# Gathering expert rows: h in PSUM, the dot products shared out over three engines, and the picks chosen between dots

## The reference

```python
def peer_ffn(h, wq, keys, u, v):       # u, v: (16384, 2048)
    q = (xt @ wq).reshape(-1, 8, 2, 128)
    s = jnp.einsum('thpc,hpnc->thpn', q, keys)
    sv, si = lax.top_k(s, 16)
    cand = (sv[:, :, 0, :, None] + sv[:, :, 1, None, :]).reshape(-1, 8, 256)
    cid = (si[:, :, 0, :, None] * 128 + si[:, :, 1, None, :]).reshape(-1, 8, 256)
    top_s, top_j = lax.top_k(cand, 16)
    eid = jnp.take_along_axis(cid, top_j, axis=-1)
    gate = jax.nn.softmax(top_s, axis=-1)
    ue = jnp.take(u, eid, axis=0)
    act = jax.nn.gelu(jnp.einsum('thkd,td->thk', ue, xt), approximate=False)
    ve = jnp.take(v, eid, axis=0)
    return jnp.einsum('thk,thkd->td', gate * act, ve)
```

## Time and profile before

| | us |
|---|---|
| median of 3 runs | 3186.89 (3186.21 to 3187.88) |
| the profiled execution, its own time | 3189.3 |
| its span, first to last instruction | 3187.6 |
| first gather of u issued | 1815.94 |
| first dot starts | 1835.04 |
| last dot's result read | 2576.1 |
| steady matmuls of the v stage from | 2644.8 |

### The profile page before, as it was taken

The page is one execution under the profiler, slowest core; times in us unless marked ns, Lnnn a source line. Parts: engine busy times, 40 slices in busy tenths (PEclk is TensorE's granted clock), DMA queues, the critical chain, the costliest instruction groups (busy, mean ns, idle before and its releaser), DMA issues.

```text
span 3187.6 us, 33891 instructions
## 1 busy us (share of the span) xinstructions
PE 2394.3 (75%) x10945; PEld 2000.4 (63%) x10945; DVE 2242.5 (70%) x2950; ACT 1111.3 (35%) x1197; POOL 763.3 (24%) x548
## 2 busy tenths in 40 slices
PE   7999999999999998999998900000111149999997
PEld 5888888888888886888886700000111147887885
DVE  4456455555444556455656699999999998888888
ACT  4444344444444543343443300000000024444443
POOL 1000000000000000000000076665565614455543
PEclk8999999999999998899999955555555589999998
DMA  7655555555656354555564498888897928999996
GB/s 246 195 186 185 178 179 191 185 192 185 185 185 185 124 194 139 164 162 166 187 221 155 172 403 369 362 362 354 316 379 306 391 78 294 320 317 331 322 323 230
DMA packets 183123, 766.51 MB, mean 240 GB/s; under 512 B 22172, under 2 KB 22224, under 8 KB 149104
## 3 DMA queue, kind: packets, MB, share of 16 engines
q1 hardware_dynamic: 123232, 415.29, 40.3%
q0 software_dynamic: 59792, 349.90, 28.0%
HBM read 763.00 MB, written 2.10 MB: 240 GB/s over the span
## 4 chain that ended last, share of the span: by engine, by line
PE 69%; DVE 22%; issue 5%; DMA 2%; ACT 1%; DVEq 1%; POOL 0%; SPq 0%; ACTq 0%; POOLq 0%
PE half L604 50%; PE half L945 15%; DVE ring L1853 14%; DVE onehot_a L1840 2%; PE half L623 1%; DMA w_raw<-in_a_w_in 1%; DMA v_raw<-in_peer_v 1%; DVE onehot_b L1836 1%; PE half L800 1%; DVEq L1840 0%; PE half L672 0%; DMA v_rows<-in_peer_v,idx 0%; DVE left L1751 0%; PE half L903 0%; DVE onehot L1794 0%
## 5 line engine op out<-in xcount | busy, mean ns | idle before, releaser
L604 PE MATMUL half<-w_split,xT 128*128 128x512 f32 x7104 | 1639.0, 392 | 15.2 <-DVE xT L1302 12.6
L604 PEld LDWEIGHTS half<-w_split,xT 128*128 128x128 f32 x7104 | 1337.9, 189 | 294.5 <-issue 8.6
L1283 DVE TENSOR_TENSOR w_split<-w_raw,w_split 128x1024 fp32r<-128x1024 f32 x592 | 722.5, 1225 | 764.1 <-ACT w_split L985 763.3
L985 ACT ACTIVATE w_split<-w_raw 128x1024 fp32r<-128x1024 f32 x592 | 626.6, 1059 | 943.4 <-PE half L604 914.1
L564 POOL DMA_INDIRECT ring<-in_peer_u,idx x256 | 480.9, 1879 | 439.5 <-DVE dots L1853 186.2
L1853 DVE CUSTOM_DVE_ANT_0 ring<-ring,h 128x2048 f32<-128x2048 f32 x256 | 570.0, 2285 | 5.0 <-issue 2.5
L945 PE MATMUL half<-v_split,w_x 128*128 128x512 f32 x2304 | 526.8, 391 | 6.1 <-ACT v_split L1235 4.4
L945 PEld LDWEIGHTS half<-v_split,w_x 128*128 128x128 f32 x2304 | 434.4, 189 | 98.3 <-issue 5.6
L929 PE MATMUL half<-onehot_a,onehot_b 128*128 128x128 f32 x512 | 94.9, 361 | 334.9 <-DVE onehot_a L1840 334.9
L578 POOL DMA_INDIRECT v_rows<-in_peer_v,idx x256 | 266.7, 1042 | 330.2 <-DVE h L1917 208.5
L929 PEld LDWEIGHTS half<-onehot_a,onehot_b 128*128 128x128 f32 x512 | 87.8, 267 | 342.2 <-DVE onehot_a L1840 342.2
(11 more groups left out here) (287 smaller groups left out, 1152.8 us busy)
## 6 DMA issues: line engine op xcount, KB each, us to landing
w_raw<-in_a_w_in SPq DMA_DIRECT2D x192, 512.0 KB, 3.5
v_raw<-in_peer_v SPq DMA_DIRECT2D x256, 384.0 KB, 5.4
w_raw<-in_b_w_in SPq DMA_DIRECT2D x128, 512.0 KB, 3.5
w_raw<-in_w_in SPq DMA_DIRECT2D x112, 512.0 KB, 3.5
w_raw<-in_a_w_out SPq DMA_DIRECT2D x64, 512.0 KB, 3.5
w_raw<-in_b_w_out SPq DMA_DIRECT2D x32, 512.0 KB, 4.3
w_raw<-in_w_out SPq DMA_DIRECT2D x32, 512.0 KB, 4.6
w_raw<-in_peer_wq SPq DMA_DIRECT2D x32, 512.0 KB, 4.3
```

What stands on the lines that cost most here:

```text
L604: last = mm(ps[half][:, 2 * t + n, :], xt[:, xp, kk, tok], w_split[:, s, wp, n * BANK:(n + 1) * BANK], start=(k == 0 and xp == 0 and wp == ...
L985: fn(w_split[:, k % SPLIT_SLOTS, 0, :], w_raw[:, k % RAW_SLOTS, :], ACT.Copy).then_inc(hi_done, 1)
L1283: v.tensor_tensor(w_split[:, s, 1, :], w_raw[:, k % RAW_SLOTS, :], w_split[:, s, 0, :].bitcast(F32), ALU.subtract).then_inc(split_done, 1)
```

## The change

It does these things to the gather stage:

- ACT copies `h` of tile 0 into `flat[B]` and of tile 1 into `flat[A]` (`h_copied`), and the dots on DVE read `h` there (new L1911). They write their sums straight to `wgt`; `dots`, `idx`, `stage` and their copies are gone.
- Of each batch of 8, rows 3 and 7 (`POOL_ROWS`) are no longer DVE's. POOL multiplies the row by `h` in SBUF (`scale_row`, new L580, 128 x 2048 f32, both inputs in SBUF), and ACT sums the product (`sum_row`, new L1228). DVE has the six others.
- POOL's queue is written out: four gathers, a `scale_row`, four gathers, a `scale_row`. The gathers read the row numbers in place in `eid`. The gather into slot 3 or 7 waits for ACT's sum of that slot, those of the others for DVE's dot.
- `choosing(n + 1)` is cut into nine pieces that stand between the dots of group n, and `finish_gate(n + 1)` follows the dot at place 21. DVE's casts and constant-operand steps in it are written as TENSOR_TENSOR with a table of constants (`ones`, `halving`).
- The one-hots beside tile 1 come once in each batch, after its second row; `onehot_a` is made by SCALAR_TENSOR_TENSOR there. The scatter products of both tiles go into half B. Keys and weights are turned together (`picks0`, `picks1`). The last quarter of `h` is weighed by ACT (`weigh_h`).

The core of the diff:

```diff
+BATCHES = PICKS // GATHER_SLOTS
+POOL_ROWS = (3, 7)
+DVE_ROWS = tuple(s for s in range(GATHER_SLOTS) if s not in POOL_ROWS)
...
-            BODY = 2 * GATHER_SLOTS
-            with pool.Fori(0, TILES * PICKS // BODY) as i:
-                for n in range(BODY):
-                    b, s = divmod(n, GATHER_SLOTS)
-                    if s == 0:
-                        pool.wait_ge(idx_ready[b], i + 1)
-                    if s == GATHER_SLOTS // 2:
-
-                        pool.wait_ge(products, CHUNKS)
-
-                    pool.wait_ge(rows_used, i * BODY + (n + 1))
+            def gather_u(r):
+
+                s = r % GATHER_SLOTS
+                if r % GROUP_PICKS == 0:
+                    pool.wait_ge(chosen, r // GROUP_PICKS + 1)
+                if r == GATHER_SLOTS // 2:
+                    pool.wait_ge(products, CHUNKS)
+                if r >= GATHER_SLOTS:
+                    j = r // GATHER_SLOTS - 1
+                    if s in POOL_ROWS:
+                        pool.wait_ge(rows_summed, j * len(POOL_ROWS) + POOL_ROWS.index(s) + 1)
+                    else:
+                        pool.wait_ge(rows_used, j * len(DVE_ROWS) + DVE_ROWS.index(s) + 1)
+                pool.nop(nofuse=True)
+                nc.gpsimd.indirect_dma_start(
+                    out=ring[:, s, :], out_offset=None, in_=peer_u_2[0],
+                    in_offset=bass.IndirectOffsetOnAxis(ap=eid[:, r:r + 1], axis=0),
+                ).then_inc(row_landed[s], 16)
+
+            def scale_row(j, s):
+
+                pool.wait_ge(row_landed[s], j * 16 + 16)
+                nc.gpsimd.tensor_tensor(ring[:, s, :], ring[:, s, :], h[:, j // BATCHES, :], ALU.mult)\
+                    .then_inc(rows_scaled, 1)
+
+            for r in range(GATHER_SLOTS):
+                gather_u(r)
+            for j in range(TILES * BATCHES):
+                s = 0
+                for last in POOL_ROWS:
+                    scale_row(j, last)
+                    while s <= last:
+                        if j + 1 < TILES * BATCHES:
+                            gather_u((j + 1) * GATHER_SLOTS + s)
+                        s += 1
...
+            is_emptied(act, "peer_q1")
+            fn(flat[B], h[:, 0, :], ACT.Copy).then_inc(h_copied, 1)
             scores_out(1)()
+            is_emptied(act, "scores1")
+            fn(flat[A], h[:, 1, :], ACT.Copy).then_inc(h_copied, 1)
+
+            def sum_row(j, s):
+
+                r = j * GATHER_SLOTS + s
+                act.wait_ge(rows_scaled, j * len(POOL_ROWS) + POOL_ROWS.index(s) + 1)
+                fn(ring[:, s, :], ring[:, s, :], ACT.Copy, accum_out=wgt[:, r:r + 1]).then_inc(rows_summed, 1)
...
+            def dot_rows(n, at):
+
+                t = n // TILE_GROUPS
+                for k in range(GROUP_PICKS):
+                    r = n * GROUP_PICKS + k
+                    j, s = divmod(r, GATHER_SLOTS)
+                    if s in DVE_ROWS:
+                        dve.wait_ge(row_landed[s], 16 * j + 16)
+                        v.tensor_tensor_reduce(out=ring[:, s, :], in0=ring[:, s, :], in1=flat[1 - t], scale=1.0,
+                                               scalar=0.0, op0=ALU.mult, op1=ALU.add,
+                                               accum_out=wgt[:, r:r + 1]).then_inc(rows_used, 1)
+                    for job in at.get(k, ()):
+                        job()
...
             for n in range(GROUPS_IN_ALL):
+                t, q = divmod(n, TILE_GROUPS)
+                at = {}
                 if n + 1 < GROUPS_IN_ALL:
-                    choose(n + 1)
+                    there, a_first, a_next, pairs, b_first, b_next, exps, key_a, key_b, ids = choosing(n + 1)
+                    at = {1: [there, a_first], 4: [a_next], 6: [pairs], 8: [b_first], 10: [b_next], 12: [exps, key_a],
+                          16: [key_b], 18: [ids], 21: [lambda: finish_gate(n + 1)]}
...
+                if t == 1:
+                    for m in range(P // SCATTER):
+                        group, k = divmod(9 + 8 * m if m + 1 < P // SCATTER else PICKS - 4, GROUP_PICKS)
```

More of the change, by code:

```diff
@@ L563, in _ @@
+            pool.wait_ge(keys_known, TILES)
+            for t in range(TILES):
+                for r in range(t * PICKS, (t + 1) * PICKS):
+                    pool.wait_ge(v_used, r + 1)
                     pool.nop(nofuse=True)
                     nc.gpsimd.indirect_dma_start(
-                        out=ring[:, s, :], out_offset=None, in_=peer_u_2[0],
-                        in_offset=bass.IndirectOffsetOnAxis(ap=idx[:, b, s:s + 1], axis=0),
-                    ).then_inc(row_landed[s], 16)
@@ L569, in _ @@
[L569 to L582 removed]
+                        out=v_rows[r % V_SLOTS][:, :], out_offset=None,
@@ L935, in _ @@
                 pe.wait_ge(keys_known, t + 1)
-                turn_picks(f"pkT{t}", [pick_keys[:, t, half, :] for half in range(2)])
                 pe.wait_ge(wgt_done, t + 1)
-                turn_picks(f"wgtT{t}", [wgt[:, t * PICKS:(t + 1) * PICKS]])
+                turn_picks(f"picks{t}", [pick_keys[:, t, half, :] for half in range(2)]
+                           + [wgt[:, t * PICKS:(t + 1) * PICKS]])
+                emptied(f"picks{t}")()
                 scatter(t)
@@ L1807, in choosing @@
                         + best16(cand, cand_left, tops, topj, GROUP_HEADS)
-                        + [exponents, look_up(0, a, ALU.logical_shift_right, 4), look_up(1, b, ALU.bitwise_and, TOPK - 1),
+                        + [exponents, look_up(0, a, ALU.logical_shift_right), look_up(1, b, ALU.bitwise_and),
                            experts])
-            def choose(n):
-                for part in choosing(n):
-                    part()
             def finish_gate(n):
@@ L1842, in one_hots @@
                 ins.then_inc(onehot_done, 1)
-            def dot_rows(n, batches=0):
-                t, q = divmod(n, TILE_GROUPS)
-                first = n * GROUP_PICKS
-                per = batches // (GROUP_PICKS // BODY)
-                with dve.Fori(0, GROUP_PICKS // BODY) as i:
-                    for b in range(2):
-                        for s in range(GATHER_SLOTS):
-                            gathered(i, first + b * GATHER_SLOTS, s)
-                            v.tensor_tensor_reduce(out=ring[:, s, :], in0=ring[:, s, :], in1=h[:, t, :], scale=1.0,
-                                                   scalar=0.0, op0=ALU.mult, op1=ALU.add,
-                                                   accum_out=dots[:, b, s:s + 1]).then_inc(rows_used, 1)
-                            done = b * GATHER_SLOTS + s + 1
-                            if done * per % BODY == BODY // 2:
-                                m = q * batches + done * per // BODY
-                                one_hots(m % 2, i * per + m, i * (per * SCATTER) + m * SCATTER)
-                        dve.wait_ge(rows_used, i * BODY + (first + (b + 2) * GATHER_SLOTS))
-                        v.tensor_copy(wgt[:, bass.ds(i * BODY + (first + b * GATHER_SLOTS), GATHER_SLOTS)], dots[:, b, :])
-                        stage(b, i * BODY + (first + (b + 2) * GATHER_SLOTS))
@@ L1870, in weights, with weights_turned @@
                 dve.wait_ge(wgt_done, t + 1)
-                step(v.tensor_scalar(h[:, t, V_DENSE:], h[:, t, V_DENSE:], ALPHA, None, ALU.mult))
-                is_emptied(dve, f"wgtT{t}")
-            dve.sem_inc(rows_used, GATHER_SLOTS)
+            def weights_turned(t):
+                is_emptied(dve, f"picks{t}")
             dve.sem_inc(v_used, V_SLOTS)
-            def first_indices():
-                for b in range(2):
-                    stage(b, b * GATHER_SLOTS)
             def keys_of(t):
@@ L1909, in _ @@
+                dot_rows(n, at)
             weights(1)
+            weights_turned(1)
             def weigh(t, i, m):
```

149 lines of the change are left out of this document (86 added, 63 removed).

## The result

The changed kernel takes 3142.55 us (3139.18 to 3144.21), the kernel before beside it 3187.39 us (3186.21 to 3190.68). The ratio is 0.986 (0.9845 to 0.9875): 45 us faster where 34 were forecast, inside the range. The profiled execution took 3142.1 us with a span of 3140.4, against 3189.3 and 3187.6.

What follows compares the result with a forecast made beforehand. DVE was taken to bound the gather stage, with nothing hidden by the v stage: 1825.7 + 340 + 376 = 2542 instead of 2576, -34 us, so 3186.9 - 34 = 3153 us; range 3085 to 3183.

Steps and rivals of the forecast that it cites:

- What bounds the program: Whole program: PE fills the v stage, so any gather-stage gain shows in full; the chain there is DVE alone.
- Start: Gather stage start: the first dot waits only for ACT's copy of h, starting at 1825.7, 9.3 us earlier.
- Prices: Gather stage instructions: dot 2.283 us, gather 0.94, POOL multiply 4.7, ACT sum 1.9 and covered, one-hots at present cost.
- Who excludes whom: DVE against POOL: two-SBUF-input DVE instructions wait up to 4.9 us for a multiply, dots with PSUM do not; chance 0.58.
- The rival with free passage: Gather stage: POOL's multiply does not hold DVE up; stage end 2481, -95 us, kernel 3092; chance 0.23.
- Tile 0: Gather stage, first tile: 69.8 us of DVE work plus 14.7 gives 85 us a group, 340 for the tile.
- The walk through a group: Gather stage, batch by batch: DVE's waits for POOL's multiplies sum to 14.6 us per group in tile 1.
- Tile 1: Gather stage, second tile: three groups of 97 us and a last of 85, 376 us against 379.7 before.
- 358 GB/s: Gather DMAs: the skill's HBM rate gives 2.93 us a row, 750 for 256, no gain; set aside for 423 GB/s.
- The middling multiply: POOL in the gather stage: a multiply of 5.5 to 6.7 us, stage 700 to 750, -0 to -30 us; chance 0.09.
- The sign of tile 1: Gather stage, second tile: forecast about equal to before, 376 us against 379.7.

Runs made afterwards that it cites:

- The first experiment: Changed kernel with DVE's dots reading h in SBUF again, the copies into PSUM left unused: 3330.39 us against 3142.55.
- The narrow multiply: Changed kernel with POOL multiplying only 256 of 2048 columns, so its result is not the program's: 3085.07 us, ratio 0.9682 to the kernel before.
- the wait of POOL for the one-hots: Changed kernel with look-ups, gate and one-hots placed later, and POOL's second multiply per tile 1 batch waiting for the one-hots: 3099.05 us, ratio 0.9729.

## Why the prediction held, and where it was off

**What bounds the program: right.** The v stage did not hide anything: 48.4 us off the stage, 47.2 off the span. One reading was wrong and carried no weight: POOL is busy 61 to 69% in the three stretches of the gather stage, not 49 to 69.

**Start: right.** 1825.31 us against 1825.7; DVE's 10.3 us of waiting for the copy of h is in the timeline.

**Prices: right.** The dot is 2283 ns with h in PSUM, the gather 0.94 us, the one-hot by SCALAR_TENSOR_TENSOR costs the same as before when undisturbed (340 to 343 ns for one, where the range had gone from half to double). POOL's multiply was worked out as 4.7 us from a fill and a mask; it is 4.53. ACT's sum held a gather up once (5.4 us, in tile 1). DVE's own work per group in tile 0 is busy 303.4 less 26 of waits, over four: 69.4 us, against 69.8.

**Who excludes whom: right.** The first experiment shows it in both directions. Two-input instructions wait and the searches that read one tensor don't; only TENSOR_SCALAR, which reads one tensor and waits all the same, was not in the rule. The Trainium skill (SBUF — State Buffer, Who interferes with whom) has the second engine blocked for the whole instruction; the trace agrees, with 32 elements that took 4.42 us beside a multiply of 4.50. The rival with free passage is out: its 3092 us is about what was measured (3085) where the multiply is short.

**Tile 0: mis-sized by 23 us, and the step that failed.** I took 85 us a group, from 69.8 of work, 11.7 of waits and 3 for landing, and so had DVE above the 79.3 us of the DMAs. Measured are 69.4, 6.6 (26.4 / 4) and 3.4 of idle DVE, 79.3 in all. The walk through a group put the multiply of POOL on the look-ups behind places 12 and 16. In tile 0 these wait for nothing (192 ns); the gate does (3.5 us in the mean), and so does the cast behind place 6 (L1826, 2.6 us in the mean), which the walk had free. The walk was made with DVE leading. In fact POOL is led by the landing of rows, as in this view of POOL's waits in tile 0:

```profile
POOL ring L580 <- DMA ring<-in_peer_u,eid: 19.0, 26, 4.6
```

I read from it that the multiplies come later against DVE's dots than I had them; no experiment took this apart. The narrow multiply shows that at this size it did not matter: tile 0 is 317 us with and without waits. The right term was the larger of the DMAs' 79.3 and DVE's sum, 317 us, where 340 stood: 23 us too much.

**Tile 1: mis-sized by 9 us.** 376 was forecast and 385.2 measured. DVE's own work was 78.4 a group in the mean and is 78.2 ((381.59 - 69) / 4). The waits are 69 us where 63 stood, and 3.6 us are idle. Their spread was wrong: 43 us lie on the one-hots, for which the walk had 31, since it had them free in half the batches. The sets of one-hots were also dealt out wrongly: four to a group, where the code has three in the first group, four in the next two and five in the last. So the first group took 90.5 us, not 97, and the last 93.0, not 85: 3.2 us of the latter are the fifth set's own work, and the rest waits, 23.6 us for 19. The two in the middle took 99.9 and 101.8, against 97. Tile 1 came out 9 us longer than forecast and tile 0 23 us shorter, which leaves the 14 us by which the forecast of the stage's end (2542 against 2527.7) was too late; the total was off by 10 to 11 us. That it was no more is in part luck, as the two errors point in opposite directions.

**358 GB/s.** The Trainium skill's figure for a core (DMA: Bandwidth & Descriptors, Specifications) does not hold here: 420 GB/s over 317 us. It had been weighed against the earlier trace rows and put aside, rightly.

**A rival's bound: wrong.** The middling multiply was given 700 to 750 us for the stage and -30 us at best. From 1825.7 a stage of 700 us ends at 2526, which is -50. With a multiply of 4.53 us the case did not arise.

**The sign of tile 1.** Tile 1 of the changed kernel is 5.5 us longer than before, though DVE has 32 dots fewer in it. The sharing takes 32 dots x 2.21 = 71 us of DVE's time off the tile and some 8 us of copies go; but one choosing more (17 us) now lies in it instead of in tile 0, and 69 us come as waits: +7 by this sum. That is where the gain went that the stage could have had: with the wait of POOL for the one-hots, 43.5 us of it come back.

What stays open is a part of the 14 us between that version and the narrow multiply. Their profiled executions are 11.9 us apart. What follows the last dot is 7.4 us longer (619.2 against 611.8), most of it the last set of one-hots behind the last dot; no run has that set before it with the rest unchanged. The stage from first dot to last is 7.8 us longer (655.8 against 648.0). The start is 3.3 us earlier (1822.1 against 1825.5), which the edit doesn't explain. 42 us of waits are left by the same count, part of them in tile 0, where they cost nothing; how the rest would split was not tried.
